# A two-part transformer block on one core: router and low-rank weights stacked side by side, the router's scores by tiles of tokens, and layer two started with a projection by rows

## The reference, cut to what matters

```python
# first block, each layer
u = h @ w_in[i]                                   # latent (mla), differential and stick-breaking parts
mix = concat([y_mla, y_diff, y_sb]) @ w_o[i]
h = layer_norm(ALPHA * h + mix, ln1_g, ln1_b)
scores = sigmoid(h @ router_w)                    # 1024 x 16, the same router in both layers
gate = two best of 16 experts, weights scores/sum # after router_b and a choice of the best group
ffn = sum over experts: gate_e * (silu(h @ w_gate[e]) * (h @ w_up[e])) @ w_down[e]
ple = sigmoid(h @ ple_gate[i]) * (p[i] @ ple_proj[i])
h = layer_norm(ALPHA * h + ffn + ple, ln2_g, ln2_b)

# second block, each layer: among its projections
lr = x @ w_in[:, GLR:GLR+16]                      # 1024 x 16
log_a = log_sigmoid(lr @ w_gate_up + b_gate) / 16
```

## Time and profile before

| | us |
|---|---|
| median of three runs | 1901.97 |
| the profiled execution, its own time | 1902.19 |
| its span, from the first to the last record | 1900.9 |
| TensorE busy | 1798.9 (95%) |
| VectorE busy | 1353.4 (71%) |
| ScalarE busy | 1132.5 (60%) |

### The profile page before, as it was taken

How to read it: one execution, slowest core, us unless ns; L and a number is a source line. 1 busy time by engine, 2 the same in 40 slices (tenths; PEclk the granted TensorE clock), 3 DMA queues, 4 the chain that set the end, 5 groups by cost and what they waited for, 6 DMA issues and landing times.

```text
span 1900.9 us, 28026 instructions
## 1 busy us (share of the span) xinstructions
PE 1798.9 (95%) x11460; PEld 1558.3 (82%) x11460; DVE 1353.4 (71%) x1603; ACT 1132.5 (60%) x1576; POOL 151.3 (8%) x152
## 2 busy tenths in 40 slices
PE   6999999999799999999989999999999999999998
PEld 5878777777697877777779889988998989989887
DVE  6777999999648689999976575655556666565555
ACT  4576778878447567878856444444444645444443
POOL 1000412200000040220000100000000000000000
PEclk9899999999899999999989999999999999999999
DMA  8334699999534469999856445555555544546552
GB/s 255 114 139 157 268 350 367 336 355 344 167 116 149 163 232 354 363 341 351 340 187 202 135 155 178 188 186 180 178 191 167 176 140 150 199 155 205 195 178 89
DMA packets 193062, 413.21 MB, mean 217 GB/s; under 512 B 16384, under 2 KB 130816, under 8 KB 176544
## 3 DMA queue, kind: packets, MB, share of 16 engines
q1 hardware_dynamic: 191840, 409.76, 62.0%
q10 hardware_dynamic: 1088, 1.57, 0.3%
HBM read 409.47 MB, written 1.84 MB: 216 GB/s over the span
## 4 chain that ended last, share of the span: by engine, by line
PE 62%; DVE 32%; ACT 3%; DMA 1%; issue 1%; POOL 0%; SPq 0%; DVEq 0%; ACTq 0%
DVE weights_lo L391 23%; PE PS L406 10%; PE PS L410 10%; PE PS L407 10%; PE PS L414 7%; PE PS L417 7%; PE PS L418 7%; ACT weights_hi L386 2%; DVE expert_rows_lo L1746 2%; PE PS L1449 1%; PE PS L433 1%; DMA weights_raw<-in_w_in 1%; PE PS L1463 1%; PE PS L1522 1%; DVE hT_lo L606 1%
## 5 line engine op out<-in xcount | busy, mean ns | idle before, releaser
L391 DVE TENSOR_TENSOR weights_lo<-weights_raw,weights_hi 128x1024 fp32r<-128x1024 f32 x564 | 661.4, 1218 | 212.7 <-ACT weights_hi L386 212.1
L386 ACT ACTIVATE weights_hi<-weights_raw 128x1024 fp32r<-128x1024 f32 x564 | 561.0, 1046 | 129.2 <-PE PS L418 74.3
L406 PE MATMUL PS<-hT_hi,weights_hi 128*128 128x256 f32 (+1 forms) x1488 | 427.3, 287 | 18.9 <-ACT weights_hi L386 12.7
L410 PE MATMUL PS<-hT_hi,weights_lo 128*128 128x256 f32 (+1 forms) x1488 | 424.4, 285 | 1.2 <-DVE weights_lo L391 1.2
L407 PE MATMUL PS<-hT_lo,weights_hi 128*128 128x256 f32 (+1 forms) x1488 | 424.2, 285 | 0.0
L406 PEld LDWEIGHTS PS<-hT_hi,weights_hi 128*128 128x128 f32 (+1 forms) x1488 | 284.9, 191 | 26.5 <-issue 20.8
L410 PEld LDWEIGHTS PS<-hT_hi,weights_lo 128*128 128x128 f32 (+1 forms) x1488 | 284.6, 191 | 2.5 <-DVE weights_lo L391 1.9
L407 PEld LDWEIGHTS PS<-hT_lo,weights_hi 128*128 128x128 f32 (+1 forms) x1488 | 284.9, 191 | 1.9
L391 DVE TENSOR_TENSOR weights_lo<-arena,weights_hi 128x1024 fp32r<-128x1024 f32 x128 | 151.0, 1221 | 17.0 <-ACT weights_hi L386 17.0
L414 PE MATMUL PS<-weights_hi,opa_hi 128*128 128x512 f32 x384 | 152.4, 397 | 3.5 <-DVE opa_lo L606 3.3
L417 PE MATMUL PS<-weights_lo,opa_hi 128*128 128x512 f32 x384 | 151.7, 395 | 0.0
(11 more groups left out here) (325 smaller groups left out, 3143.4 us busy)
## 6 DMA issues: line engine op xcount, KB each, us to landing
weights_raw<-in_w_in SPq DMA_DIRECT2D x80, 1024.0 KB, 5.7
weights_raw<-in_w_ff SPq DMA_DIRECT2D x64, 1024.0 KB, 5.3
weights_raw<-in_w_up SPq DMA_DIRECT2D x34, 1024.0 KB, 6.8
weights_raw<-in_w_down SPq DMA_DIRECT2D x34, 1024.0 KB, 7.2
weights_raw<-in_w_gate SPq DMA_DIRECT2D x30, 1024.0 KB, 7.0
arena<-in_w_down SPq DMA_DIRECT2D x30, 1024.0 KB, 6.8
arena<-in_w_gate SPq DMA_DIRECT2D x18, 1024.0 KB, 7.1
params<-in_w_gate SPq DMA_DIRECT2D x16, 1024.0 KB, 7.2
```

Of the source, the lines that this page charges most:

```text
L386: act.activation(u.flat[0][:, c:e], u.x[:, c:e], ACT.Copy).then_inc(*sig.mark("w_hi", u.u, i))
L391: dve.tensor_tensor(u.flat[1][:, c:e], u.x[:, c:e], u.flat[0][:, c:e].bitcast(F32), ALU.subtract).then_inc(*sig.mark("w_lo", u.u, i))
L406: pe.matmul(o, w[0], x[0], start=start, stop=False)
L410: return pe.matmul(o, w[1], x[0], start=False, stop=stop)
```

## The change

1. **Stacked weights.** High and low part of the router's (and the low-rank gate's) weights lie side by side in one tile of 32 columns. One matmul by the high part of the activations and one by the low part give all four products: rows 0 to 15 of the result are of the high weights, rows 16 to 31 of the low ones.
2. **Router.** It goes tile by tile: 16 matmuls of 128 moving columns for tile 0, then the wait for `T11`, then 16 for tile 1. ScalarE copies the 32 x 256 raw sums; TensorE multiplies them by a folding matrix (32 x 16), which turns and adds the halves; ScalarE applies the sigmoid to that, and VectorE's copy goes.
3. **Low-rank gate.** 16 matmuls of 256 columns in place of 24; `w_gate_up` is loaded twice, one copy under the other, so that the following matmul adds the halves.
4. **Layer 1** starts with `mla 0`: its plan order, the feeds of ScalarE and VectorE, and TensorE. Its first tile is computed between the turning of tile 0 and of tile 1. `up_params` of layer 1 moves to before `diff q1`'s load, the third unit.
5. **`w_o 1`** waits for `y lo 0` and only at its second tile for `y lo 1`.

```diff
     for l in range(DEPTH):
         w = a["w_in"][l]
+        if l > 0:
+            cols("mla 0", w, 0)
         pair("diff q", w, MLA_W)
         pair("diff k", w, MLA_W + 512)
-        cols("mla 0", w, 0)
+        if l == 0:
+            cols("mla 0", w, 0)
...
-        rw_s = (sb("rw_hi", [P, KD, 16], F32R), sb("rw_lo", [P, KD, 16], F32R))
-        lr_s = rw_s
+        rw_both = sb("rw_hi_lo", [P, KD, 32], F32R)
+        rw_s = lr_s = (rw_both[:, :, 0:16], rw_both[:, :, 16:32])
...
+        def product_stacked(pe, o, both, y, start, stop):
+            pe.matmul(o, both, y[0], start=start, stop=False)
+            return pe.matmul(o, both, y[1], start=False, stop=stop)
...
-        def project_rows(pe, label, names, n, x, by, among=8, at=None, between=None):
+        def project_rows(pe, label, names, n, x, by, among=8, at=None, between=None, norm=None):
+            if norm:
+                keep_clock(pe, banks.turn % among, 8)
+                turn_tile(pe, norm, 0)
...
                 u = use(pe, name)
+                if norm:
+                    keep_clock(pe, banks.turn % among, 4)
                 for t in range(NT):
+                    if norm and t:
+                        turn_tile(pe, norm, 1)
                     for k in range(u.k):
                         kk = k0 + k
+                        if norm and kk % 4 == 0:
+                            pe.wait_ge(*sig.at("dve_took", f"{norm} T{t}{kk // 4}"))
...
-            pe.wait_ge(*sig.at("diff_dve", n_("y lo 1")))
-            accumulate_rows(pe, L("w_o 1", "w_o 2"), opa, 2, n_("ln1"), True, False)
+            pe.wait_ge(*sig.at("diff_dve", n_("y lo 0")))
+            accumulate_rows(pe, L("w_o 1"), opa, 2, n_("ln1"), True, False,
+                            midway=lambda: pe.wait_ge(*sig.at("diff_dve", n_("y lo 1"))))
+            accumulate_rows(pe, L("w_o 2"), opa, 4, n_("ln1"), False, False)
...
             turn_tile(pe, n_("ln1"), 1)
-            pe.wait_ge(*sig.at("dve_took", n_("ln1") + " T11"))
...
-            for k in range(KD):
-                last = product3(pe, PS[0:16, b, 0:S], at_k(rw_s, k, 0, 16), at_k(hT, k, 0, S), k == 0, k == KD - 1)
+            for t in range(NT):
+                if t:
+                    pe.wait_ge(*sig.at("dve_took", n_("ln1") + " T11"))
+                for k in range(KD):
+                    last = product_stacked(pe, PS[0:32, b, t * P:(t + 1) * P], rw_both[:, k, :],
+                                           at_k(hT, k, t * P, (t + 1) * P), k == 0, k == KD - 1)
...
-                last = transpose(pe, PS[:, b, 16 * t:16 * t + 16], scT[0:16, t * P:(t + 1) * P])
+                last = pe.matmul(PS[:, b, 16 * t:16 * t + 16], scT[0:32, t * P:(t + 1) * P], const[0:32, C_FOLD16:C_FOLD16 + 16],
+                                 start=True, stop=True)
...
-            act.activation(scT[0:16, :], PS[0:16, banks.of(n_("router")), 0:S], ACT.Sigmoid).then_inc(
+            act.activation(scT[0:32, :], PS[0:32, banks.of(n_("router")), 0:S], ACT.Copy).then_inc(
                 *sig.mark("act_took", n_("router")))
+            act.wait_ge(*sig.at("ps", n_("router T")))
+            act.activation(sc, PS[:, banks.of(n_("router T")), 0:32].rearrange("p (t e) -> p t e", t=NT), ACT.Sigmoid).then_inc(
+                *sig.mark("act_took", n_("router T")))
...
-            dve.wait_ge(*sig.at("ps", n_("router T")))
-            step(dve, "dve_took", dve.tensor_copy(sc, PS[:, banks.of(n_("router T")), 0:32].rearrange("p (t e) -> p t e", t=NT)),
-                 n_("router T"))
+            dve.wait_ge(*sig.at("act_took", n_("router T")))
...
-                last = product3(pe, PS[0:16, b, 0:S], at_k(lr_s, k, 0, 16), at_k(hT, k, 0, S), k == 0, k == KD - 1)
+                last = product_stacked(pe, PS[0:32, b, 0:S], rw_both[:, k, :], at_k(hT, k, 0, S), k == 0, k == KD - 1)
...
-            if name == "mla 0":
+            if name == ("diff q1" if l else "mla 0"):
                 if l == 0:
                     lambda_sync(sp)
                 up_params(sp, l)
```

More of the change, by code:

```diff
@@ L39 @@
            mybir.EngineType.Pool)
[L41 to L43 removed]
+C_IDENT, C_TRI, C_ONES, C_SBKEEP, C_SBNEG, C_CAUSAL, C_CHUNK, C_SCAN, C_COL, C_RANK, C_SWAP, C_IOTA, C_FOLD, C_FOLD16 = (
+    0, 128, 256, 384, 512, 640, 768, 832, 1088, 1096, 1112, 1144, 1272, 1272 + SLOTS)
+N_CONST = 1272 + SLOTS + 16
 COL_INV1, COL_INV2, COL_SIGN, COL_NHALF, COL_PART, COL_STEP = range(6)
@@ L915, in tensor_block1 @@
             n_ = lambda name: f"{name} {l}"
-            pe.wait_ge(*(sig.at("xT_dve", 1) if l == 0 else sig.at("dve_took", f"ln2 {l - 1} T11")))
+            if l == 0:
+                pe.wait_ge(*sig.at("xT_dve", 1))
+            else:
+                project_rows(pe, n_("mla 0"), L("mla 0"), 256, hT, "act_took", among=4, norm=f"ln2 {l - 1}")
             project_T(pe, L("diff q0"), hT, "act_took")
@@ L922, in tensor_block1 @@
             take_steps(tables, 2)
-            project_rows(pe, n_("mla 0"), L("mla 0"), 256, hT, "act_took")
+            if l == 0:
+                project_rows(pe, n_("mla 0"), L("mla 0"), 256, hT, "act_took")
             take_steps(tables, 2)
@@ L1069, in scalar_block1, with first_rows @@
             into = lambda dst: lambda view, c: copy(dst[:, c:c + 2, :], view)
+            def first_rows():
+                rows_takes(act, feed, n_("mla 0"), L("mla 0"), "act_took", lambda view, t: copy(crow[:, t, 0:256], view[:, 0:256]))
+            if l > 0:
+                first_rows()
             project_takes(act, feed, L("diff q0"), "act_took", into(dqT))
@@ L1079, in scalar_block1 @@
             take_steps(tables, 2)
-            rows_takes(act, feed, n_("mla 0"), L("mla 0"), "act_took", lambda view, t: copy(crow[:, t, 0:256], view[:, 0:256]))
+            if l == 0:
+                first_rows()
             take_steps(tables, 2)
@@ L1197, in vector_block1 @@
             copy = dve.tensor_copy
+            if l > 0:
+                feed(n_("mla 0"))
             feed(n_("diff q0"))
@@ L1205, in vector_block1 @@
             take_steps(tables, 4)
-            feed(n_("mla 0"))
+            if l == 0:
+                feed(n_("mla 0"))
             take_steps(tables, 1)
@@ L1414, in tensor_experts @@
             pe.wait_ge(*sig.at("act_took", n_("router")))
-            b = banks.take(pe, n_("router T"), "dve_took", among=4)
+            b = banks.take(pe, n_("router T"), "act_took", among=4)
             for t in range(NT):
-                last = transpose(pe, PS[:, b, 16 * t:16 * t + 16], scT[0:16, t * P:(t + 1) * P])
+                last = pe.matmul(PS[:, b, 16 * t:16 * t + 16], scT[0:32, t * P:(t + 1) * P], const[0:32, C_FOLD16:C_FOLD16 + 16],
+                                 start=True, stop=True)
             last.then_inc(*sig.mark("ps", n_("router T")))
@@ L1926, in tensor_block2 @@
             for hd in range(4):
-                last = pe.matmul(two_banks(b)[:, hd, :], lr_up[:, hd * P:(hd + 1) * P], lrT[0:16, :], start=True, stop=True)
+                last = pe.matmul(two_banks(b)[:, hd, :], lr_up[:, hd * P:(hd + 1) * P], lrT[0:32, :], start=True, stop=True)
             last.then_inc(*sig.mark("ps", n_("gate pre")))
@@ L2063, in scalar_block2 @@
             act.wait_ge(*sig.at("ps", n_("lr T")))
-            copy(lrT[0:16, :], PS[0:16, banks.of(n_("lr T")), 0:S]).then_inc(*sig.mark("act_took", n_("lr T")))
+            copy(lrT[0:32, :], PS[0:32, banks.of(n_("lr T")), 0:S]).then_inc(*sig.mark("act_took", n_("lr T")))
             feed(n_("gla k1"))
@@ L2427, in sync_program @@
             x_in(sp)
-            first, ends = NRAW, [place["diff q0 1"] + NRAW, place["gla v0 0"] + NRAW]
+            first, ends = NRAW, [place["mla 0 1"] + NRAW, place["gla v0 0"] + NRAW]
             load_unit(sp, units[0])
```

9 lines of the change are left out of this document (4 added, 5 removed).

## The result

| | before | after |
|---|---|---|
| median of four runs, us | 1902.44 | 1886.92 (1885.31 to 1888.14) |
| ratio, 95% interval | | 0.9917 [0.9905, 0.9929] |
| profiled execution, its own time, us | 1902.19 | 1888.14 |
| its span, us | 1900.9 | 1886.9 |

Predicted were 1892.8 us, between 1888.5 and 1899.

What follows compares the result with a forecast made beforehand. TensorE, busy 95% of the span, was taken as the bound, with VectorE's chain deciding at the router. 1.2 + 2.7 + 1.85 + 3.4 = 9.15 us off 1901.97 gave 1892.8 us, range 1888.5 to 1899.

Steps and rivals of the forecast that it cites:

- What lies between passes it on: Whole kernel: stretches between the edited places hand each gain on in full, so the terms add to 9.15 us.
- `w_o 1`, 1.2 us: Start of `w_o 1`: TensorE starts 0.6 us earlier in each of two layers, 1.2 us, between 0 and 1.3.
- Router, 2.7: Router in both layers: the choice of experts begins 1.37 us earlier in each, 2.7 us; 0.2 to 1.55 per layer.
- the row at 223.25: Profile row where a table load begins while TensorE is still transposing; read as the sigmoid's load running ahead of the wait.
- narrow passes: Router rival: 128 moving columns cost 0.233 us a matmul, the choice begins 3.3 us later per layer, 1902.1 us; 8%.
- table load waits: Router rival: the sigmoid's table load stands behind the new wait, 2 x 1.2 us less gain, 1895.1 us; 10%.
- the fallen clock: Routers and low-rank gates, rival: narrow products bring the clock down, costing 16 us, 1909 us; 4%.
- Low-rank gate, 1.85: Low-rank gate: 16 matmuls for 24 save 0.93 us each time, twice, 1.85 us; bounds 1.6 and 2.0.
- Layer 1, 3.4: Start of layer 1: `mla 0` fills idle time, then `diff q1`'s load limits; 3.4 us, bounds 0.7 and 5.2.
- Tile 1's turning keeps its time: Start of layer 1: tile 1's turning, set by VectorE's norm, comes no later than before.
- the load is later: Layer 1 rival: `diff q1`'s load lands in 9.8 us, total gain 6.5 us, 1895.5 us; 10%.
- the sum for the half clock: Layer 1: with the clock at half until 517, TensorE's matmuls through `diff q0` end at 522.7 instead of 520.6.

Runs made afterwards that it cites:

- e1: Kernel before with one unused tile of 64 bytes per partition behind the constants, no instruction changed: 1896.88 us, ratio 0.9970.
- e4: Changed kernel with its folding matrix in a tile of its own behind all others, so addresses as before: 1891.73 us, ratio 0.9939.
- e11: Kernel before with only the stacked router, its folding and the stacked low-rank gate, addresses as before: 1898.75 us, ratio 0.9968.
- e3: Kernel before with an unused tile of 96 bytes behind the constants: 1896.72 us, ratio 0.9965.
- e6: Kernel before with an unused tile of 32 bytes ahead of all tiles, the weights' buffers too: 1902.67 us, ratio 0.9994.
- f4: Kernel before with its small tiles relb, steps_hi and lam in front of h, distance 192, no instruction changed: 1882.72 us, ratio 0.9881.
- e8: Kernel before with only the new start of layer 1 in the first block, addresses as before: 1900.15 us, ratio 0.9986.
- e10: Changed kernel with layer 1's norm wait and three small parameter loads before diff k1's load, not diff q1's: 1884.16 us, ratio 0.9886.
- e7: Changed kernel with four small tiles between its large ones, so that opa begins at a multiple of 128 bytes: 1880.1 us, ratio 0.9875.

## Why the prediction was wrong, step by step

- **The step that failed** is the sum's silent one: "What lies between passes it on", with every untouched matmul priced as in the trace of before ("at 0.118 each"). I costed each instruction of the diff, and took the wider constants for free (`N_CONST`, 16 columns more for the folding matrix). They moved `hT` and `opb` from distance 224 to 32, the 256-column step from 118.3 to 116.8 ns, and the second block, where TensorE never rests, gave 7.8 instead of 1.85 us. In the profiled executions that block takes 922.9 us before, 916.3 with the move alone (e1), 920.3 with the change alone (e4) and 915.1 with both. The move alone gave 6.2 us (1903.06 less 1896.88); with it the forecast would have been 1886.6. The medians of e1 and e4 would add up to 17.5, not 15.5; within their intervals that is the same.
- **`w_o 1`, 1.2 us:** right by the trace (0.6 in layer 0, 0.45 in layer 1); not run alone, so its worth in the total isn't shown.
- **Router, 2.7:** right up to the slots, 1.31 and 1.26 us earlier, forecast 1.37; the table load stood where the row at 223.25 said. "What lies between passes it on" held only in part here: the experts gave 0.6 and 0.3 us back (0.6 and 0.45 in e11's trace). In the changed kernel's layer 0 the clock was at half for 6.8 us there, for 3.4 before; what takes the rest wasn't followed. The rivals "narrow passes" and "table load waits" fall (0.061 us a matmul), and so does the fallen clock: in the changed kernel's trace no clock fall begins at a router's or a low-rank gate's matmuls.
- The row for 128 columns had to come from 64-column ones, and held. The Trainium skill (TensorE: Matmul & The Clock Gate, Back-to-back issue gap) gives about 81 ns for 128 moving columns; with a stationary operand of 32 columns this trace has 60 ns. No run here has 128 columns there in the split format.
- **Low-rank gate, 1.85:** right, 16 steps of 0.113 for 24 of 0.116.
- **Layer 1, 3.4:** the mechanism was right (24 matmuls before the second turning, then `diff q1`'s load). One premise failed in the changed kernel's trace: "Tile 1's turning keeps its time" (1.9 us later, counted from the norm's start, with the clock at half). Kernels with the old order show such a norm too (e3 12.5 us, e6 11.8, f4 11.7), and some with the new one don't (e8 and e10, 10.9), so it isn't shown to be the edit's doing. From the start of the last expert's last matmul to the layer's first rotation the eleven kernels with the old start took 53.6 to 55.8 us (mean 54.6), the five with the new one 50.1 to 55.1 (mean 52.0): 2.6 us, as the run alone (2.7). Part of the scatter is the clock: in e7 it fell once more right behind the stop of `diff q1`, and the stretch took 55.1. The four kernels without that stop took 49.4 to 51.2, mean 50.0, 2.0 less; three of them have other steps too, so this isn't the load's price alone (e10, with the changed kernel's addresses: 49.4 against 51.1).
- **Rival "the load is later"**: in the trace's own time its low part came 0.3 us off the forecast, by two errors that cancel: issued 1.9 us late after the norm, landed in 6.0 us for 7.0. Counted from the norm's start it came 0.9 us late. The long landing of 9.8 wasn't seen.
- **In the sum for the half clock** 522.7 should read 522.9 by the rows' own rate (18 matmuls in 3.94 us); nothing hangs on it.

## What to carry to other kernels

A change to the size or order of on-chip tiles is a change to every matmul that reads them: in a kernel bound by TensorE, compare the step of matmuls that the diff doesn't touch first, and try an unused tile of 32 to 224 bytes before any cleverer edit (here: from 9 us slower to 20 faster). Measure a change at unmoved addresses as well, or an address gain is taken for the edit's, and the next edit to a table takes it away. In a queue, a load that a stage needs early goes ahead of small loads that wait for a distant event.

## What the runs showed of the hardware

- The step of a 256-column matmul in this split format depends on where its two operands lie: 115.4 to 119.9 ns, one of 512 columns 227 to 234. Changing only the distance between the tiles moved the kernel by 29 us (1882.72 to 1911.85). Why the distance counts wasn't found. The Trainium skill (SBUF — State Buffer, SBUF: two separate sides) says that TensorE never waits for another engine's accesses. The traces agree: the step is the same with the other engines at work or idle (118.4 and 118.3 ns before); it goes with the place of TensorE's own two operands.
- At distances 64 and 192 the step has two levels, 113 to 114 and 118 ns, and keeps one over many units. In f4's trace the first and last of 192 matmuls, at two places of the second block's layer 1: 191 steps in 21.77 us (114.0 ns) and in 22.58 (118.2).

```profile
1464.18 0.39 PE L407 MATMUL PS<-hT_hi,weights_hi 128*128 128x256 f32 x1
...
1485.95 0.28 PE L411 MATMUL PS<-hT_hi,weights_lo 128*128 128x256 f32 x1
...
1630.84 0.36 PE L407 MATMUL PS<-hT_hi,weights_hi 128*128 128x256 f32 x1
...
1653.42 0.28 PE L411 MATMUL PS<-hT_hi,weights_lo 128*128 128x256 f32 x1
```

What chooses the level stays open; held at the lower one throughout, it would be worth at most some 8 us more, an estimate from 4294 x (115.4 - 113.5) ns.
